# A Mamba-2 layer with MoE on one core: transposed chunk scan, decay rows and clamp on ScalarE, no state terms at a group's ends

## What is computed

```python
a = -jnp.exp(a_log) * dt
x_dt = xs * dt
a_cum = jnp.cumsum(a, axis=-1)                       # within a chunk
decay = jnp.exp(segsum(a))                           # exp(a_cum[l] - a_cum[s]), s <= l
cb = jnp.einsum('bclgn,bcsgn->bcgls', cc, bc)
y_diag = jnp.einsum('bcgls,bgrcls,bcsgrp->bclgrp', cb, decay, x_dt)
decay_states = jnp.exp(a_cum[..., -1:] - a_cum)
states = jnp.einsum('bclgn,bgrcl,bclgrp->bcgrpn', bc, decay_states, x_dt)
# state entering a chunk: the states before it, decayed
y_off = jnp.einsum('bclgn,bcgrpn,bgrcl->bclgrp', cc, states, jnp.exp(a_cum))
y = (y_diag + y_off) + xs * d_skip
yg = rms_norm((y * silu(z)) per group) ; out = yg @ w_out
```

## Time and profile before

| | |
|---|---|
| median of 3 runs | 1704.89 us |
| the profiled execution's own time | 1698.84 us |
| its span, first to last instruction | 1697.1 us |
| TensorE busy | 1586.0 us, 93% |
| VectorE, ScalarE, GpSimd busy | 76%, 42%, 36% |
| mean granted TensorE clock | 0.969 |

### The profile page before, as it was taken

How to read it: one execution, slowest core, us unless ns; L and a number is a source line. 1 busy time by engine, 2 the same in 40 slices (tenths; PEclk the granted TensorE clock), 3 DMA queues, 4 the chain that set the end, 5 groups by cost and what they waited for, 6 DMA issues and landing times. The chain is left out here.

```text
span 1697.1 us, 26206 instructions
## 1 busy us (share of the span) xinstructions
PE 1586.0 (93%) x7462; PEld 1277.6 (75%) x7462; DVE 1286.7 (76%) x2319; ACT 708.3 (42%) x1203; POOL 612.6 (36%) x754
## 2 busy tenths in 40 slices
PE   6999999999999999999999882799999999999996
PEld 5778888878888788888888772577777777777774
DVE  6658868768778688687786757687888788878883
ACT  5333232322233232322332330566666666566652
POOL 2222121131221312211302111246667665766664
PEclk9999999999999999999999885799999999999998
DMA  4121221121121212211212635699999999999981
GB/s 152 44 77 50 54 70 36 50 70 44 57 69 44 59 49 53 73 35 53 71 42 63 220 118 199 233 338 371 369 371 373 368 374 367 377 375 370 380 324 57
DMA packets 142991, 292.67 MB, mean 172 GB/s; under 512 B 21340, under 2 KB 71948, under 8 KB 142896
## 3 DMA queue, kind: packets, MB, share of 16 engines
q1 hardware_dynamic: 127904, 266.29, 44.9%
q0 software_dynamic: 14992, 25.22, 4.1%
HBM read 291.81 MB, written 25.30 MB: 187 GB/s over the span
## 5 line engine op out<-in xcount | busy, mean ns | idle before, releaser
L1845 DVE TENSOR_TENSOR gu_lo<-w_gu,gu_hi 128x1024 fp32r<-128x1024 f32 x256 | 305.6, 1224 | 65.1 <-ACT gu_hi L1719 43.9
L1027 PE MATMUL proj<-uTh,wl 128*128 128x512 f32 x768 | 311.0, 405 | 6.8 <-issue 6.8
L1029 PE MATMUL proj<-uTh,wh 128*128 128x512 f32 x768 | 302.5, 394 | 0.0
L1028 PE MATMUL proj<-uTl,wh 128*128 128x512 f32 x768 | 302.4, 394 | 0.0
L1719 ACT ACTIVATE gu_hi<-w_gu 128x1024 fp32r<-128x1024 f32 x256 | 261.5, 1056 | 83.8 <-PE g_ps L1782 32.5
L450 POOL TENSOR_TENSOR wl<-raw,wh 128x512 fp32r<-128x512 f32 x96 | 129.1, 1363 | 390.1 <-ACT wh L511 390.1
L1027 PEld LDWEIGHTS proj<-uTh,wl 128*128 128x128 f32 x768 | 146.4, 191 | 37.3 <-issue 7.4
L1029 PEld LDWEIGHTS proj<-uTh,wh 128*128 128x128 f32 x768 | 146.0, 190 | 31.9
L1028 PEld LDWEIGHTS proj<-uTl,wh 128*128 128x128 f32 x768 | 146.6, 191 | 28.8
L564 ACT ACTIVATE xbc<-v 128x512 f32<-128x512 f32 x64 | 40.5, 633 | 297.3 <-DVE v L847 297.3
L847 DVE SCALAR_TENSOR_TENSOR v<-xr,cw,v 128x512 f32<-128x512 f32 x192 | 146.1, 761 | 15.7 <-DVE v L847 1.5
(11 more groups left out here) (259 smaller groups left out, 3311.6 us busy)
## 6 DMA issues: line engine op xcount, KB each, us to landing
w_gu<-in_moe_w_gate_dram SPq DMA_DIRECT2D x128, 512.0 KB
w_gu<-in_moe_w_up_dram SPq DMA_DIRECT2D x128, 512.0 KB
w_d<-in_moe_w_down_dram SPq DMA_DIRECT2D x128, 512.0 KB
raw<-in_ssd_w_in_dram SPq DMA_DIRECT2D x96, 256.0 KB, 3.5
E<-acum_dram SPq DMA_DIRECT2D x64, 256.0 KB, 3.5
raw<-in_ssd_w_out_dram SPq DMA_DIRECT2D x32, 256.0 KB, 2.9
hacc<-in_x_dram SPq DMA_DIRECT2D x8, 512.0 KB, 7.5
u_dram<-xbc SPq DMA_DIRECT2D x8, 512.0 KB, 3.3
```

What stands on the lines that cost most here:

```text
L1027: nc.tensor.matmul(out, al, bh, start=start, stop=False)
L1028: nc.tensor.matmul(out, ah, bl, start=False, stop=False)
L1029: return nc.tensor.matmul(out, ah, bh, start=False, stop=stop)
L1845: vec.tensor_tensor(wl[:, j % RING, :], weights.gate_up(b, j), wh[:, j % RING, :].bitcast(F32), ALU.subtract).then_inc(w_lo, 1)
```

## The change

1. `scan` writes y transposed (channels on partitions), so that `turn_y` and its wait go. The state term takes two matmuls with S as weights and 128 columns each, in place of one with 256 columns. The four products with the decay take x·dt (64 columns) as weights and E (128 columns) as the moving side, and write partitions 0 to 63 or 64 to 127.
2. VectorE's factor for the state term is no longer a number per partition (`eac`) but a row per head, exp(a_cum), spread over the head's 64 partitions: `EE`, made by ScalarE in two instructions of 64 partitions from the loaded rows (`decay_rows`).
3. `sub_e` leaves VectorE. ScalarE computes relu(a_cum[s] - row) for each of the four heads, and exp of the negative (`decay_between`).
4. These stand behind the copies of A and of B's tile, ahead of the early pieces (in c = 1 behind the first two). `exp_e` stood ahead of the copy of A.
5. Chunk 0 of a group has no state term, and its state is a copy; the last chunk (7) of a group has no transpose and copy of B, no `xds`, no state update, no memsets.

```diff
-            def exp_e(G, c):
-                wait(act, sub_steps, G, 32, 4 * c + 4)
+            def decay_rows(G, c):
+                wait(act, e_loaded[c % 2], G, 16 * NT // 2, 16 * (c // 2 + 1))
+                if c % NT == 0:
+                    return
+                wait(act, y_steps, G, 2 * NT - 1, 2 * (c - 1) - 1 if c > 1 else 0)
+                for h in range(2):
+                    half_p = slice(h * HEAD_DIM, (h + 1) * HEAD_DIM)
+                    rows_h = E[half_p, c % 2].rearrange("p (t q) l -> p q t l", q=2)[:, h]
+                    nc.scalar.activation(EE[half_p, c % 2], rows_h, ACT.Exp).then_inc(ee_done, 1)
+
+            def decay_between(G, c):
+                a = pick(acum, G) if c < 8 else pick(acum, nxt(G))
+                if c % NT:
+                    wait(act, ee_done, G, 2 * (NT - 1), 2 * states(c))
+                for r in range(R):
+                    er = E[:, c % 2, r, :]
+                    nc.scalar.activation(er, er, ACT.Relu, bias=a[:, 0, c % 8, r:r + 1], scale=-1.0).then_inc(relu_done, 1)
+                wait(act, relu_done, G, 32, 4 * c + 4)
                 e = E[:, c % 2].rearrange("p r l -> p (r l)")
-                nc.scalar.activation(e, e, ACT.Exp).then_inc(exp_done, 1)
+                nc.scalar.activation(e, e, ACT.Exp, scale=-1.0).then_inc(exp_done, 1)
...
@@ ScalarE, body
-                    if c < NT - 1 or not last:
-                        exp_e(G, c + 1)
                     A = unit_of(G, plan[c][0]) if plan[c] else None
...
                     if c < NT - 1 or not last:
                         copy_b(G, c + 1)
+                        decay_rows(G, c + 1)
+                        decay_between(G, c + 1)
                     for q in early[c][2 if c == 1 else 0:]:
                         piece(G, *q)
...
@@ VectorE
-            def sub_e(G, c):
-                wait(dve, e_loaded[c % 2], G, 16 * NT // 2, 16 * (c // 2 + 1))
-                a = pick(acum, G) if c < 8 else pick(acum, nxt(G))
-                for r in range(R):
-                    e = E[:, c % 2, r, :]
-                    vec.tensor_scalar(e, e, a[:, 0, c % 8, r:r + 1], 0.0, ALU.subtract, ALU.min).then_inc(sub_steps, 1)
...
-                vec.tensor_tensor(heads(ysb[:]), heads(y_ps[:, 0, :]), spread(eac, G, c), ALU.mult).then_inc(y_steps, 1)
+                if c % NT == 0:
+                    vec.tensor_copy(ysb[:], y_ps[:, 1, :]).then_inc(y_steps, 1)
+                    return
+                vec.tensor_tensor(ysb[:], y_ps[:, 0, :], EE[:, c % 2].rearrange("p t l -> p (t l)"), ALU.mult
+                                  ).then_inc(y_steps, 1)
...
@@ VectorE, gate
-                wait(dve, yT_done, G, NT, k + 1)
+                wait(dve, y_steps, G, 2 * NT - 1, 2 * k + 1)
                 for t in range(2):
                     vec.scalar_tensor_tensor(ygf[:, t, :], xbc[:, par, t, cols], dsk[:, bass.ds(val(G, 2, t), 1)],
-                                             st_ps[:, 1, t * P:(t + 1) * P], ALU.mult, ALU.add).then_inc(gate_steps, 1)
+                                             ysb[:, t * P:(t + 1) * P], ALU.mult, ALU.add).then_inc(gate_steps, 1)
...
@@ TensorE, scan
-                wait(pe, s_steps, G, 2 * NT, 2 * c)
-                wait(pe, y_steps, G, 2 * NT, 2 * c)
-                nc.tensor.matmul(y_ps[:, 0, :], xbc[:, H[1] % 2, 3, cc * P:cc * P + P], S[:, c % 2, :], start=True, stop=True)
+                wait(pe, y_steps, G, 2 * NT - 1, 2 * c - 1)
+                if c % NT:
+                    wait(pe, s_steps, G, 2 * (NT - 1), 2 * c)
+                    for t in range(2):
+                        nc.tensor.matmul(y_ps[:, 0, t * P:(t + 1) * P], S[:, c % 2, t * P:(t + 1) * P],
+                                         xbc[:, H[1] % 2, 3, cc * P:cc * P + P], start=True, stop=True)
                 wait(pe, m_done, G, NT, c + 1)
                 for r in range(R):
                     q = slice(r * HEAD_DIM, (r + 1) * HEAD_DIM)
-                    mm = nc.tensor.matmul(y_ps[:, 1, q], E[:, c % 2, r, :], xdt[:, c % 2, q], start=True, stop=True)
+                    half_p = slice(r % 2 * HEAD_DIM, (r % 2 + 1) * HEAD_DIM)
+                    mm = nc.tensor.matmul(y_ps[half_p, 1, r // 2 * P:(r // 2 + 1) * P], xdt[:, c % 2, q], E[:, c % 2, r, :],
+                                          start=True, stop=True)
                 mm.then_inc(y_mm, 1)
+                if c == NT - 1:
+                    return
...
-            def turn_y(G, c):
-                wait(pe, y_steps, G, 2 * NT, 2 * c + 2)
-                wait(pe, s_steps, G, 2 * NT, 2 * c + 2)
-                for t in range(2):
-                    mm = nc.tensor.transpose(st_ps[:, 1, t * P:(t + 1) * P], ysb[:, t * P:(t + 1) * P], ident[:])
-                mm.then_inc(yT_done, 1)
```

More of the change, by code:

```diff
@@ L655, in _ @@
                 if i == 6:
-                    exp_e(G0, 0)
+                    decay_rows(G0, 0)
+                    decay_between(G0, 0)
             copy_b(G0, 0)
-            exp_e(G0, 1)
+            decay_rows(G0, 1)
+            decay_between(G0, 1)
             copy_b(G0, 1)
@@ L877, in prep @@
             def prep(G, c):
-                wait(dve, btok_done, G, NT, c + 1)
+                if c == NT - 1:
+                    wait(dve, tcb_done, G, NT, c + 1)
+                else:
+                    wait(dve, btok_done, G, NT - 1, states(c) + 1)
                 wait(dve, y_mm, G, NT, c - 1)
@@ L895, in make_m, with y_sum, state @@
                 vec.tensor_tensor(E[:, c % 2], E[:, c % 2], cb, ALU.mult).then_inc(m_done, 1)
-            def y_and_state(G, c, last_chunk):
+            def y_sum(G, c):
                 wait(dve, y_mm, G, NT, c + 1)
-                wait(dve, yT_done, G, NT, c)
-                vec.tensor_tensor(heads(ysb[:]), heads(y_ps[:, 0, :]), spread(eac, G, c), ALU.mult).then_inc(y_steps, 1)
-                wait(dve, y_steps, G, 2 * NT, 2 * c + 1)
-                vec.tensor_tensor(ysb[:], ysb[:], y_ps[:, 1, :], ALU.add).then_inc(y_steps, 1)
-                new = S[:, (c + 1) % 2, :]
-                wait(dve, st_mm, G, NT, c + 1)
-                if last_chunk:
+                wait(dve, gate_steps, G, 24, 3 * c)
+                if c % NT == 0:
+                    vec.tensor_copy(ysb[:], y_ps[:, 1, :]).then_inc(y_steps, 1)
+                    return
+                vec.tensor_tensor(ysb[:], y_ps[:, 0, :], EE[:, c % 2].rearrange("p t l -> p (t l)"), ALU.mult
+                                  ).then_inc(y_steps, 1)
+                wait(dve, y_steps, G, 2 * NT - 1, 2 * c)
+                vec.tensor_tensor(ysb[:], ysb[:], y_ps[:, 1, :], ALU.add).then_inc(y_steps, 1)
+            def state(G, c):
+                if c == NT - 1:
+                    return
+                new, update = S[:, (c + 1) % 2, :], st_ps[:, 0, :]
+                wait(dve, st_mm, G, NT - 1, states(c) + 1)
+                if c % NT == 0:
                     for j in range(2):
-                        vec.memset(new[:, j * P:(j + 1) * P], 0.0).then_inc(s_steps, 1)
+                        vec.tensor_copy(new[:, j * P:(j + 1) * P], update[:, j * P:(j + 1) * P]).then_inc(s_steps, 1)
                     return
-                wait(dve, s_steps, G, 2 * NT, 2 * c)
+                wait(dve, s_steps, G, 2 * (NT - 1), 2 * c)
                 vec.tensor_tensor(heads(new), heads(S[:, c % 2, :]), spread(dch, G, c), ALU.mult).then_inc(s_steps, 1)
-                wait(dve, s_steps, G, 2 * NT, 2 * c + 1)
-                vec.tensor_tensor(new, new, st_ps[:, 0, :], ALU.add).then_inc(s_steps, 1)
+                wait(dve, s_steps, G, 2 * (NT - 1), 2 * c + 1)
+                vec.tensor_tensor(new, new, update, ALU.add).then_inc(s_steps, 1)
             def gate(G, k):
@@ L958, in _ @@
             make_m(G0, 0)
-            sub_e(G0, 1)
             prep(G0, 1)
-            y_and_state(G0, 0, False)
+            y_sum(G0, 0)
+            state(G0, 0)
             make_m(G0, 1)
@@ L975, in body @@
                         conv_unit(*prev_b)
-                    if more:
-                        sub_e(G, c + 1)
                     gated_low(G, k)
@@ L985, in body @@
                     if c < NT or not last:
-                        y_and_state(G, c, c == NT - 1)
+                        y_sum(G, c)
+                        state(G, c)
                     if more:
@@ L1066, in tcb @@
                 wait(pe, unit_final, H, NU, 7 if cc < 4 else 8)
-                wait(pe, xdt_steps, G, 2 * NT, 2 * (c - 1))
-                wait(pe, btok_done, G, NT, c - 1)
+                wait(pe, xdt_steps, G, 2 * NT - 1, c - 1 + states(c - 1))
+                wait(pe, cbm_done, G, NT, c - 1)
+                wait(pe, btok_done, G, NT - 1, states(c - 1))
                 out = tcb_ps[c % 2]
-                for t in range(3):
+                for t in range(2 if c == NT - 1 else 3):
                     nc.tensor.transpose(out[:, t, :], xbc[:, par, t, cols], ident[:])
@@ L1192, in body @@
```

(2 more changed lines are left out.)

31 lines of the change are left out of this document (16 added, 15 removed).

## The result

The changed kernel takes **1713.51 us** (median of 5, 1712.82 to 1720.78) against 1704.89 (1703.48 to 1707.07): a ratio of 1.005, 95% interval 1.0034 to 1.0067. It is slower by 0.5%, where I forecast 0.35% faster, 1699. The range of 1683 to 1716 holds the time; the direction is wrong.

The account below looks back on a forecast made before the run. TensorE's instructions plus its waits bound the loop. Terms -26.9 + 3 + 21.7 - 3.5 + 1 - 3.5 + 3 = -5.2, some -6 with hidden savings, gave 1693 us profiled, 1699 median; range 1683 to 1716.

Parts of the forecast that it names:

- the waits for the square: TensorE waiting for ScalarE's square of the gated y in iterations 3, 5 and 7: to shrink by 3.5 us in 7 groups.
- Matmuls removed: TensorE's turn, state term, state update and B's transpose, dropped or made shorter: -26.9 us together.
- Products: TensorE's eight product instructions with the decay, now half-width: +0.05 us per chunk, +3 us in all.
- rival 1: The two halves of the products overlap on TensorE: 8 to 17 us less, 1691 to 1682; chance 0.16.
- ScalarE's decay: ScalarE's new rows, clamps and exponential per chunk: 2.95 us, or 2.1 in iteration 7.
- Weight waits: TensorE waiting for GpSimd's low parts of the weights, 1.7 us in iteration 6 and 1.4 in 7: +21.7 us in 7 groups.
- The masked decay: VectorE needs it behind y and state; exponential ends about 3.4 us after the sum of squares' start, a tie counted as nothing.
- The start: At the loop's start, the wait for the first state and the slow clock behind it go: -3.5 us.
- The clock behind the weight waits: TensorE's clock falls behind 2 of the 14 new waits for weights, at 1.6 us each: +3 us.
- rival 2: The clock falls at the weight waits: all 12 further falls give 1718, six give 1709; chance 0.18.
- The last group: Bound by the chain to the gate, not matmuls: only some 1.3 us of its 2.3 us savings come out, +1 us.

Follow-up runs that it names:

- e7: The changed kernel, but GpSimd computes only a quarter of the low parts of weight tiles 2 and 3; ratio 0.9847 to the kernel before.
- e4: The changed kernel, but the decay's clamp is on VectorE again, behind prep and the mean square; ratio 1.0254 to the kernel before.
- e9: The changed kernel, but in iterations 6 and 7 alone the early weight pieces stand ahead of the decay on ScalarE; ratio 0.9916 to the kernel before.
- e10: The changed kernel, but the state term is computed a head at a time, with 64 columns of weights, like the products; ratio 1.0014 to the kernel before.
- e8: The changed kernel, but the products of all four heads are written to the same half of the partitions; ratio 1.0109 to the kernel before.
- e11: The changed kernel with y in PSUM and the early weight pieces ahead of the decay, run again; ratio 0.978 to the kernel before.
- e12: The changed kernel with y in PSUM, early pieces ahead of the decay, and weight pieces moved to where VectorE has time; 1655.31 us, ratio 0.9705 to before.
- e2: The changed kernel, but ScalarE makes the early weight pieces right behind the copy of B, ahead of the decay; ratio 0.9842 to the kernel before.
- e1: The changed kernel, but the finished y is written to PSUM and the gate reads it there; ratio 0.9995 to the kernel before.

## Why the prediction was wrong

**The step that failed** is the one on the waits for the square: "In iteration 7 the wait goes under the one for weights (0.3), in 5 about 0.2 goes, in 3 none: -3.5 us in 7 groups." They grew by 11.5 us, a miss of 15, and TensorE's clock fell behind nine of them, 14 us where I had 3 for all falls. The prediction's reason was that the chain from B's copy to the gate "starts earlier". In iterations 2 and 4, whose chains end in the waits of 3 and 5, it does not: `xdt` starts 1.38 and 0.70 us behind the sum of squares, 1.18 and 0.59 before.

I had seen that the early pieces become late, and asked only who waits for the weights. I did not ask what GpSimd and VectorE do to each other when the pieces move. The trace of before had it: `xds` at 1.48 beside GpSimd (the row of 166.92 above), 0.42 elsewhere. That the gate's y moves from PSUM to SBUF stood in the diff, and I gave it no term.

In iteration 4 the two sides of the wait can be read apart. From the sum of squares (165.78 before, 162.85 after) to the gate's end VectorE needed 11.28 us and now 12.07, and TensorE's own work up to the next sum of squares took 11.23 and now 10.93. The first grew by 0.8, the second shrank by 0.3, and the wait grew by both, from 0.39 to 1.48. Of the 0.8, 0.5 is the longer stops (1.3 to 1.8); the rest is the later start of `xdt` (0.1) and a later y (0.1). From 2 to 3 the gate's end comes 0.76 later: 0.4 is the longer stop at the gate, 0.2 the later `xdt`, 0.2 the mask, which now waits for the exponential. So the stops are the larger part in one place and half in the other. e7 shows how far they reach: with most of them out, both periods end below those of the kernel before.

"It frees VectorE of 0.87 us a chunk, which is worth little: VectorE then waits for B's copy anyway" holds for the kernel before. e4 adds that the clamp would cost much if it stood inside the chain.

The other terms, in the order of the forecast:

- *Matmuls removed:* the turn and the update came as priced: in e9, without weight waits, 7→8 is 0.80 us shorter than before, which fits 0.22 of the turn, 0.49 of the update and 0.09 of the three steps below. B's transpose is not to be told apart. The **state term** was forecast at 0.44 and takes 0.62, the update 0.04 to 0.05 more than before: the change of form, which I had charged to the products, falls mostly ahead of them (e10).
- *Products:* forecast 0.89 from one step of form to the next, measured 0.59, under the 0.6 that I had set as a sign of being wrong. The halves overlap; this is rival 1's mechanism, and e8 speaks for it (1.02 with one half). Together state term, products and update are 0.09 per chunk shorter where I had 0.02, 4 us in 56 chunks. That the sum is so near is luck: errors of 0.3 and 0.2 in opposite directions. The Trainium skill ("TensorEngine Tiling (Array Packing)", Key Properties) has a change of mode drain the engine; the rows agree that a change costs time, 0.18 us behind the state term and 0.07 behind the sum of squares in e10.
- *ScalarE's decay:* rows 0.84, clamps 1.28, exponential 0.63, 2.92 us from first to last, forecast 2.95. Right.
- *Weight waits:* 1.68 us in iteration 6 to 7 (1.50 in the last one) and 0.97 to 1.35 in 7, forecast 1.7 and 1.4; 19.9 us in the fourteen, forecast 21.7. Right, and e9 gives them back at their price.
- *The masked decay, a tie that I counted at nothing:* nearly. The exponential ends 3.37 us behind the sum of squares in iteration 4, forecast 3.4, and is in time; in iterations 2, 3 and 5 VectorE is idle for 0.1 us ahead of the mask.
- *The start:* forecast -3.5, measured -4.8 at the first sum of squares.
- *The clock behind the weight waits:* forecast 2 falls in 14, measured none; rival 2 did not happen. The falls came behind the square, and each cost 1.57 us (forecast 1.6). No rival had named that wait.
- *The last group:* forecast 1.3 us shorter, measured 0.1 (72.7 us from its first sum of squares to its last, 72.6 now).

The balance, read from the traces: from the first sum of squares to the last the kernel before takes 882.0 us and the changed one 900.2. TensorE's idle time in it grew from 26.0 to 55.4 us: 11.5 for the square, 19.9 for the weights, and 2.4 less in the two pauses at the loop's back edge. The granted clock stood at half for 23.9 us before and 58.0 now; that costs some 16 us, an estimate from the nine falls of 1.57 us each. What is left, -27, is the matmuls' own work; the forecast had -24, or -28 with the three steps as measured. With the earlier start, 4.8, the last sum of squares comes 13.4 us later.

The medians of the whole program differ by 8.6 only. The stage behind the loop varies by more than the 5 us between the two figures (692 to 714 us), and that stays open. That the range held the time is no merit of the forecast: 26 us too little for the square and the clock was partly made up by terms that came out shorter.

## What to carry to other kernels

When an engine's work moves in time, list what it will now run beside, not only who waits for it: for GpSimd in SBUF, each instruction of VectorE in that window that reads only SBUF. A row that is two or three times as long as its siblings in the trace of before may be such a meeting; look at what GpSimd does at its end. It shows the price before anything is changed. Put helper work that others can stop, or that stops others, into iterations where the engine it meets has a unit's time to spare; here that alone (e11 to e12) gave 12 us and the order of two calls (e2) 35.

## What the runs showed of the hardware

- **VectorE beside GpSimd.** While GpSimd computes a low part (two operands in SBUF, 1.35 us each on average), an instruction of VectorE on SBUF alone that starts after it is held and ends 0.15 to 0.55 us behind its end, whenever it began: 0.42 became 1.48 (`xds`), 0.54 became 1.53 (one tensor and two scalars), 0.60 for a pair became 2.02. Four `xds` that began ahead of GpSimd's instruction kept their 0.42 in the kernel before. Instructions with a tensor in PSUM kept their time, and moving one operand to PSUM (e1) removed the effect on that instruction wholly, 348 ns at most in 128. The Trainium skill ("SBUF — State Buffer", SBUF: two separate sides, and Who interferes with whom) says that the two share a port pair as an exclusive lock, for an instruction of VectorE with two SBUF inputs or in a two-port mode. The trace agrees for those with two inputs, and also in that the loser is stopped, not slowed; whether the convolution's first instruction, with one tensor, ran in such a mode no row here says.
- **Half-width matmuls side by side.** fp32 matmuls with 64 columns of weights, to alternate halves of the output's partitions, take 0.59 us for eight rows, and 1.02 when all go to one half (e8).
- **The clock** of the changed kernel fell behind nine of the fourteen waits for the square in iterations 3 and 5: behind nine of the twelve from 1.15 to 1.56 us, and behind neither of 0.66 and 0.89. It fell behind none of the weight waits of 0.97 to 1.68 us. What tells these apart was not tried.
